# Weight tiles stored as they lie on chip, and a new order of the modulation tiles, in a two-block transformer kernel on one Trainium2 core

## What is computed

```python
# first block, per layer; sc = silu(c), c has 1024 entries
mod = sc @ w_mod[layer] + b_mod[layer]          # w_mod: 1024 x 6144 a layer
shift1, scale1, gate1, shift2, scale2, gate2 = split(mod, 6)
h = rmsnorm(x, g_attn) * (1 + scale1) + shift1
x = x + gate1 * mixer(h)      # h @ w_in, 16 heads of three kinds of attention, @ w_out
h = rmsnorm(x, g_mlp) * (1 + scale2) + shift2
u, g = split(h @ w_up, 2)     # 1024 x 5632
x = x + gate2 * ((silu(conv(g)) * u) @ w_down)  # 2816 x 1024
# second block, per layer
x = x + mixer2(rms_norm(x)) @ w_out_2           # w_in_2: 1024 x 2336, w_uq_2, w_ukv_2
x = x + expert_choice_moe(rms_norm(x))          # 16 experts, three 1024 x 1024 matrices each
```

## Time and profile before

| | us |
|---|---|
| median of 3 runs | 1885.98 |
| range of these | 1884.85 to 1887.53 |
| profiled execution: its own time | 1892.49 |
| profiled execution: span of the trace | 1890.6 |
| PE busy | 1609.9 (85%) |
| DVE busy | 762.4 (40%) |
| ACT busy | 312.3 (17%) |
| POOL busy | 190.2 (10%) |

### The profile page before, as it was taken

The page is one execution under the profiler, slowest core; times in us unless marked ns, Lnnn a source line. Parts: engine busy times, 40 slices in busy tenths (PEclk is TensorE's granted clock), DMA queues, the critical chain, the costliest instruction groups (busy, mean ns, idle before and its releaser), DMA issues.

```text
span 1890.6 us, 24872 instructions
## 1 busy us (share of the span) xinstructions
PE 1609.9 (85%) x10540; PEld 924.4 (49%) x10540; DVE 762.4 (40%) x1518; ACT 312.3 (17%) x820; POOL 190.2 (10%) x177
## 2 busy tenths in 40 slices
PE   8999999998999999999875856767999875866757
PEld 3456998443589964474332322322474432232322
DVE  5776687768637676666000100002576000000001
ACT  2161111021511201262000000002252000000000
POOL 0020052000214410320000000000220000000000
PEclk9999999999999999999987978979999996878979
DMA  9985996443566443747999999999946999999998
GB/s 369 371 320 178 326 345 226 134 162 149 190 218 195 179 154 118 228 179 315 424 433 428 429 431 422 434 429 403 296 179 272 425 432 428 429 430 424 432 430 342
DMA packets 152386, 600.52 MB, mean 318 GB/s; under 512 B 22368, under 2 KB 81248, under 8 KB 127712
## 3 DMA queue, kind: packets, MB, share of 16 engines
q1 hardware_dynamic: 152046, 598.58, 80.6%
q10 hardware_dynamic: 242, 0.53, 0.1%
HBM read 595.28 MB, written 3.82 MB: 317 GB/s over the span
## 4 chain that ended last, share of the span: by engine, by line
PE 60%; DMA 24%; another core or an unknown queue 7%; SPq 4%; DVE 2%; ACT 1%; issue 1%; POOL 0%; DVEq 0%; ACTq 0%
DMA far<-in_w_gate 13%; PE ps L1740 11%; PE ps L1377 10%; PE ps L1403 7%; DMA far<-in_w_down 6%; PE ps L1337 4%; PE ps L1446 4%; PE ps L1205 3%; PE ps L1287 3%; PE ps L1760 3%; PE ps L1618 3%; PE ps L1477 3%; DMA ring<-in_w_gate 2%; PE ps L1053 2%; DMA ring<-in_w_mod 2%
## 5 line engine op out<-in xcount | busy, mean ns | idle before, releaser
L1740 PE MATMUL ps<-ring,near 128*32 128x256 f32 x2560 | 192.2, 467 | 96.1 <-DMA ring<-in_w_up 48.2
L3458 DVE TENSOR_TENSOR near<-ps,near 128x512 f32<-128x512 f32 x16 | 10.7, 671 | 488.8 <-PE ps L1740 488.8
L1740 PEld LDWEIGHTS ps<-ring,near 128*32 128x32 f32 x2560 | 94.8, 133 | 187.1 <-DMA ring<-in_w_up 54.0
L2538 DVE CUSTOM_DVE_ANT_0 ring<-ring,far 128x1024 f32<-128x1024 f32 x96 | 120.2, 1301 | 42.5 <-DMA ring<-in_w_mod 42.4
L1760 PE MATMUL ps<-far,near 128*32 128x512 f32 x448 | 94.4, 673 | 49.1 <-DMA far<-in_w_down 49.1
L1740 PE MATMUL ps<-far,near 128*32 128x256 f32 x1024 | 82.3, 492 | 48.9 <-DMA far<-in_w_gate 25.3
L1377 PE MATMUL ps<-near,ring 128*128 128x128 f32 x960 | 115.5, 276 | 0.0
L1377 PEld LDWEIGHTS ps<-near,ring 128*128 128x128 f32 x960 | 111.9, 193 | 0.1
L1337 PE MATMUL ps<-near,ring 128*128 128x128 f32 (+1 forms) x704 | 99.3, 303 | 0.0
L1337 PEld LDWEIGHTS ps<-near,ring 128*128 128x128 f32 x704 | 94.0, 191 | 5.9 <-issue 1.0
L3474 DVE COPY near<-ps 128x512 f32<-128x512 f32 x8 | 5.5, 691 | 210.8 <-PE ps L1760 209.0
(11 more groups left out here) (369 smaller groups left out, 2451.1 us busy)
## 6 DMA issues: line engine op xcount, KB each, us to landing
ring<-in_w_gate SPq DMA_DIRECT2D x22, 4096.0 KB, 48.6
ring<-in_w_up SPq DMA_DIRECT2D x14, 4096.0 KB, 52.8
far<-in_w_down SPq DMA_DIRECT2D x14, 4096.0 KB, 52.9
ring<-in_w_up SPq DMA_DIRECT2D x44, 1024.0 KB, 11.9
ring<-in_w_mod SPq DMA_DIRECT2D x20, 2048.0 KB, 14.2
far<-in_w_gate SPq DMA_DIRECT2D x8, 4096.0 KB, 49.2
ring<-in_w_down SPq DMA_DIRECT2D x8, 4096.0 KB, 52.4
near<-in_w_down SPq DMA_DIRECT2D x8, 4096.0 KB, 52.4
```

Source lines behind the costliest of these rows:

```text
L1740: last = mm(ps[2 * part + e // 2][j * CAP:(j + 1) * CAP, e % 2 * 2 * P:(e % 2 + 1) * 2 * P], xsT[:, k, e * CAP:(e + 1) * CAP], expert_row( ...
L2538: nc.vector.tensor_tensor_reduce(v, v, csilb, 1.0, cc1(l, "b_mod", o, 1), ALU.mult, ALU.add, col)\
```

## The change

First, each weight outside the experts is stored on the host tile by tile, so that a partition's share of a tile is one run in DRAM: 16 KB for a whole tile, 8 KB or 4 KB for the pieces of the head. One DMA loads a tile where there were two (`up`, `head_mods`, pieces of `in` in the second block, `w_uq_2` with `w_ukv_2`). The forget gate's columns become 192 bytes a partition and the router's weights 1 KB. The same bytes are moved.

Second, the mod tiles take other places in the order of loads and of reads. In layer 0, one mod tile fewer is read ahead of the attention (five, tiles 4 to 8), tile 9 and `ab` come behind it, and the tiles behind that move by one; the two halves of tile 10 stand between the residuals. Loads of mod tiles behind the attention alternate with the up tiles. In layer 1, the reading of tile (1,4) moves behind `forget_log`.

```diff
-MOD_AT = {3: (4, 5), 4: (6, 7), 5: (8, 9)}
-MOD_READ = {2: (4,), 3: (5,), 4: (6, 7), 5: (8, 9)}
+MOD_AT = {3: (4,), 4: (5,), 5: (6, 7, 8, 9)}
+MOD_READ = {3: (4,), 4: (5, 6), 5: (7, 8)}
...
-MOD_AFTER = ({("in", LAST_IN): (10,), ("out", 1): (11,), ("up", 0): (12,), ("up", 1): (13,), ("up", 2): (14, 15), ("up", 3): (16,),
-              ("up", 4): (17, 18), ("up", 8): (19,)}, {("in", LAST_IN): (0, 1), ("out", 1): (2, 3)})
-MOD_WHOLE = {0: (15,), 1: (16,), 2: (17,), 3: (18,)}
-MOD_PARTS = {6: (19, range(0, 2)), 7: (19, range(2, 4))}
+MOD_AFTER = ({("in", LAST_IN): (10,), ("out", 1): (11,), ("up", 1): (12, 13), ("up", 2): (14,), ("up", 3): (15,),
+              ("up", 4): (16,), ("up", 5): (17,), ("up", 6): (18,), ("up", 7): (19,)}, {("in", LAST_IN): (0, 1), ("out", 1): (2, 3)})
+MOD_WHOLE = {0: (14,), 1: (15,), 2: (16,), 3: (17,)}
+MOD_PARTS = {5: (18, range(0, 2)), 6: (18, range(2, 4)), 7: (19, range(0, 2)), 8: (19, range(2, 4))}
...
             def mod_tile(t):
 
                 L, _, j = B1_TILES[t]
-                v = a["w_mod"][L, j * N:(j + 1) * N, :]
-                src = v.rearrange("(p n) k -> p n k", n=4) if j // 2 in (2, 5) else v.rearrange("(n p) k -> p n k", p=P)
-                sp.dma_start(slot_at(t).rearrange("p (n k) -> p n k", n=4), src).then_inc(arrived[b1_slot(t)], 16)
+                sp.dma_start(slot_at(t), a["w_mod"][L, j]).then_inc(arrived[b1_slot(t)], 16)
...
-                ks = slice(2 * h, 2 * h + 2)
-                src = a["w_in"][0, :, IN1_ORDER[i] * N:(IN1_ORDER[i] + 1) * N].rearrange("(k p) n -> p k n", p=P)
+                v = slice(2 * h * N, 2 * (h + 1) * N)
                 sem = arrived[b1_slot(t)] if h == KD // 2 - 1 else sems[HEAD_ROWS[HEAD_IN + h - 1 if h else i]]
-                sp.dma_start(slot_at(t).rearrange("p (k n) -> p k n", k=KD)[:, ks, :], src[:, ks, :]).then_inc(sem, 16)
+                sp.dma_start(slot_at(t)[:, v], a["w_in"][0, IN1_ORDER[i], :, v]).then_inc(sem, 16)
...
-                sp.dma_start(fgate[:, l * KD * CH:(l + 1) * KD * CH].rearrange("p (k n) -> p k n", k=KD),
-                             a["w_in"][l, :, IN1:IN1 + CH].rearrange("(k p) n -> p k n", p=P)).then_inc(sems["rows_loaded"], 16)
+                sp.dma_start(fgate[:, l * KD * CH:(l + 1) * KD * CH], a["w_forget"][l]).then_inc(sems["rows_loaded"], 16)
...
                 elif kind == "up":
-                    for half in range(2):
-                        o = half * DFF + j * 256
-                        src = a["w_up"][L, :, o:o + 256].rearrange("(k p) n -> p k n", p=P)
-                        sp.dma_start(d8[:, :, half * 256:half * 256 + 256], src).then_inc(sem, 16)
+                    sp.dma_start(dst, a["w_up"][L, j]).then_inc(sem, 16)
...
                     weights_sum("t4", 1)
-                    modulation(0, range(0, 1))
                     joined(3, 0)
-                    modulation(0, range(1, 3))
                     joined(4, 0)
                     rotate("A", 16, 16)
...
                     forget_log()
+                    modulation(0, range(0, 1))
                     joined(3, 1)
+                    modulation(0, range(1, 3))
                     joined(4, 1)
...
-                if L == 0:
-                    ab(0, 1, "g_mlp")
-
...
-                modulation(2 if L else 10)
+                modulation(2 if L else 9)
+                if L == 0:
+                    ab(0, 1, "g_mlp")
                 dve.wait_ge(sems["gate_loaded"], 32 * L + 16)
                 out_residual(0, 0)
-                if L:
-                    modulation(3, range(0, 2))
+                modulation(3 if L else 10, range(0, 2))
                 out_residual(0, 1)
                 norm_stream(which, 0)
-                modulation(3 if L else 11, range(2, 4) if L else range(0, 2))
+                modulation(3 if L else 10, range(2, 4))
                 out_residual(1, 0)
...
+    arrays["w_up"] = layers(lambda l: _np.stack([rows_first(_np.concatenate([i["w_up"][l][:, o:o + 256] for o in (256 * j, DFF + 256 * j)], axis=1))
+                                                 for j in range(UPT)]))
```

More of the change, by code:

```diff
@@ L443, in two_blocks @@
         for t, tile in enumerate(B1_TILES):
-            seen[b1_slot(t)] += 32 if tile[1] == "up" or 2 <= t < FAST else 16
+            seen[b1_slot(t)] += 16
             B1_ARR.append(seen[b1_slot(t)])
@@ L447, in two_blocks @@
             for t, (kind, j) in enumerate(B2_TILES):
-                seen[b2_slot(t)] += 48 if kind == "small" else 16 * len(IN2_TILES[j][1]) if kind == "in" else 16
+                seen[b2_slot(t)] += 32 if kind == "small" else 16
                 B2_ARR.append(seen[b2_slot(t)])
@@ L813, in _ @@
                                  rpad[0:84, :].unsqueeze(1).to_broadcast([84, GRID, P])).then_inc(sems["rpb_copied"], 16)
[L814 to L815 removed]
+                    sp.dma_start(router[:, 0:DEPTH * KD * EXP], a["w_router_2"]).then_inc(sems["router_loaded"], 16)
                 slot_free(t)
@@ L820, in _ @@
                     load_gate(0, 0)
-                if (L, kind, j) == (1, "mod", 3):
+                if (L, kind, j) == (0, "up", 3):
                     store_gate(0, 1, first_block[0].at("b1_mod_read", 8))
-                if (L, kind, j) == (1, "mod", 6):
+                if (L, kind, j) == (0, "up", 4):
                     load_gate(0, 1)
@@ L2892, in _ @@
                 if L == 0:
-                    modulation(11, range(2, 4))
+                    modulation(11, range(0, 2))
                 out_residual(1, 1)
@@ L2896, in _ @@
                 if L == 0:
-                    modulation(12, range(0, 2))
+                    modulation(11, range(2, 4))
                 evac_stream(which, 1, 24)
                 if L == 0:
-                    modulation(12, range(2, 4))
+                    modulation(12)
                     modulation(13)
-                    modulation(14)
                 def conv(j):
@@ L3573, with rows_first @@
         "g_final": i["g_final"].reshape(1, D), "c": i["c"].reshape(1, D),
-        "w_mod": _np.ascontiguousarray(i["w_mod"].transpose(0, 2, 1)),
     }
-    for n in ("w_in", "w_out", "w_up", "w_down", "w_in_2", "w_out_2", "w_uq_2", "w_ukv_2",
-              "w_router_2", "conv_w_2"):
-        arrays[n] = i[n]
-    arrays["w_out_2"] = _np.ascontiguousarray(i["w_out_2"].reshape(DEPTH, KD, P, D)[:, OUT2_ROWS]).reshape(DEPTH, D, D)
+    def rows_first(v):
+        return v.reshape(v.shape[0] // P, P, v.shape[1]).transpose(1, 0, 2).reshape(P, -1)
@@ new lines, in outputs_first, with head_first, layers @@
+    def outputs_first(v, q):
+        if q // 2 in (2, 5):
+            return v.T[q * N:(q + 1) * N].reshape(P, 4 * D)
+        return v.T[q * N:(q + 1) * N].reshape(4, P, D).transpose(1, 0, 2).reshape(P, 4 * D)
+    def head_first(v, q):
+        return v.T[0:2 * D].reshape(2, KD, P, D).transpose(2, 1, 0, 3)[:, 2 * q:2 * q + 2].reshape(P, 4 * D)
+    def layers(f):
+        return _np.ascontiguousarray(_np.stack([f(l) for l in range(DEPTH)]))
+    arrays["w_mod"] = layers(lambda l: _np.stack([head_first(i["w_mod"][l], q) if l == 0 and q < FAST else outputs_first(i["w_mod"][l], q)
+                                                  for q in range(12)]))
@@ new lines @@
+    arrays["w_in"] = layers(lambda l: _np.stack([rows_first(i["w_in"][l][:, j * N:(j + 1) * N]) for j in range(IN1 // N)]))
+    arrays["w_forget"] = layers(lambda l: rows_first(i["w_in"][l][:, IN1:IN1 + CH]))
+    arrays["w_out"] = layers(lambda l: _np.stack([rows_first(i["w_out"][l][:, j * N:(j + 1) * N]) for j in range(2)]))
+    arrays["w_up"] = layers(lambda l: _np.stack([rows_first(_np.concatenate([i["w_up"][l][:, o:o + 256] for o in (256 * j, DFF + 256 * j)], axis=1))
+                                                 for j in range(UPT)]))
@@ new lines @@
+    arrays["w_down"] = layers(lambda l: rows_first(i["w_down"][l]))
+    arrays["w_in_2"] = layers(lambda l: _np.concatenate(
+        [rows_first(_np.concatenate([i["w_in_2"][l][:, o:o + w] for o, w in pieces], axis=1)) for _, pieces in IN2_TILES], axis=1))
+    out2 = i["w_out_2"].reshape(DEPTH, KD, P, D)[:, OUT2_ROWS].reshape(DEPTH, D, D)
+    arrays["w_out_2"] = layers(lambda l: _np.stack([rows_first(out2[l][:, j * N:(j + 1) * N]) for j in range(2)]))
+    arrays["w_small_2"] = layers(lambda l: _np.concatenate([rows_first(i["w_uq_2"][l]), i["w_ukv_2"][l]], axis=1))
@@ L3580 @@
+    arrays["w_router_2"] = _np.ascontiguousarray(_np.concatenate([rows_first(v) for v in i["w_router_2"]], axis=1))
+    arrays["conv_w_2"] = i["conv_w_2"]
     for n in ("w_gate_2", "w_up_2", "w_down_2"):
```

42 lines of the change are left out of this document (12 added, 30 removed).

## The result

The changed kernel takes 1876.5 us (median of 7 runs, 1875.19 to 1881.22) where the kernel before, measured beside it, takes 1887.53 (7 runs). The ratio is 0.9941, interval 0.9927 to 0.9956: 11.1 us less, 8.3 to 13.8. That lies in the range 1861 to 1877, but only 0.5 us inside its upper end, and outside the 1865.5 to 1872.5 that the forecast itself had; it is 8.1 us above its 1868.4, of which 1.5 us is the base (1885.98 then, 1887.53 beside this run). The profiled execution took 1876.95 us, its span is 1874.9.

A forecast was written before the change was run, and what follows sets the result against it. Expert weights' DMA bounds 889 to 1310, untouched; before it, PE's stalls are the gain. 1.5 + 3.5 + 4.1 + 8.5 = 17.6 us off the median 1885.98 gives 1868.4 us, range 1861 to 1877 (the forecast's own 1865.5 to 1872.5).

The forecast's parts named there:

- the second rival: A new DVE wait in up tiles or fifth `in` step takes half back; 1874 to 1878 us, chance 0.16.
- the four places: PE's stalls ahead of 889: the head, then at 70, 245 and 430 us; 17.6 us to gain in all.
- Stall 4: At 430, layer 1: DVE waits for mod tile (1,4); moving `modulation(0)` behind `forget_log` gains 8.5 us, bounds 6.8 and 8.5.
- Stall 2: At 70, `in` loop: DVE copies the third result late behind `modulation(4)`; the new order gains 3.5 us.
- Stall 3: At 245, first up tile by seven products lands late; packing and earlier issue gain 4.1 us, bounds 2.3 and 4.1.
- The head: Before 28.91, PE waits 1.17 and 0.71 us for `w_in`; faster transfers gain 1.5 us, bounds 0 and 2.9.
- What is added: Mod reads moved between residuals, behind attention, into up tiles 5 to 8: hidden; four half tiles cost 0, bound 4 us.
- The clock: Lower PE clock behind stalls 2, 3 and 4, taken as their price: 1.45, 1.74 and 1.63 us.
- The first rival: Order alone works, runs of 512 B suffice, the head gives 0: 16.1 us gained, 1869.9 us, chance 0.12.

The follow-up runs named there:

- e1_unchanged: The kernel before, run and traced a second time with nothing changed: 1886.56 us, ratio 1.000.
- e7_mod0_only: The kernel before with one edit, the reading of mod tile (1,4) moved behind the forget gate's logarithm: 1878.54 us.
- e3_layout_only: The kernel before with only the packed tiles and their loads, order of mod tiles as before: 1879.46 us.
- the spread one: The changed kernel with mod tile 18's first half ahead of the rows' sums, its second in up tile 6, tile 19 in up tiles 8 and 9: 1873.5 us.
- e5_pool_small: The changed kernel with POOL's sums of layer 0's up tiles 6 to 10 cut to 1 of 128 columns: stage "seven" 75.04 us instead of 78.50.
- e8_fill: The kernel before with unread 128x512 products filling PE's waits at stalls 2, 3 and 4: 1886.40 us against 1887.07 beside it.

## Why the prediction was right or wrong

**Where the time went.** Right: the gain was to be had only where PE stands still ahead of 889, and the experts' rate stayed. The start of the experts moved by 16.3 us between the two first traces (889.60 to 873.31), the span by 15.7. Against e1_unchanged it moved by 8.0. The medians, 11.1, lie between.

That the time lies in the range is in part luck. It fell into the second rival's band (1874 to 1878, chance 0.16), and its mechanism was at work; the outer range held it by 0.5 us in one measurement and by 0.1 in the other (1876.90). The direction and three of the four places were right by their causes.

**Stall 4**, 8.5 us: right; 8.5 by e7_mod0_only in the median, where the interval of 5.5 to 11.5 makes the exact hit luck, and 7.3 to 9.0 by the traces.

**Stall 2**, 3.5 us: gone, and its size is 2.7 against e1_unchanged and 4.0 against the first trace. I gave it to the order; e3_layout_only shows that the layout removes it as well. The margins in the later steps of the `in` loop held: PE has no wait on DVE there. (The 13.8 us for an `in` tile were added up wrongly: 2 × 7.13 − 0.2 is 14.1, and the rival has 13.7. Nothing hangs on it.)

**Stall 3**, 4.1 us: gone, as said by both parts, and either alone is enough. Up tile 5 has landed when POOL's sums begin at 220.38, before 230 as forecast. It is worth 2.5 us in a stage without a dip (77.48 to 75.03) and 4.2 with one (79.24).

**The head**, 1.5 us: nothing came. The rate rose as said (350 to 387) and the hole closed, but the two waits stayed at 1.3 and 0.6, which is the lower bound (0) that I had written down. The `w_in` waits of the head are 0.9 to 1.9 us in traces with the old layout and 0.4 to 2.1 with the new one, so no part of the 1.5 can be seen. The forget gate's loads were to be issued in under 1 us; packed they take 6.94:

```profile
27.16 6.94 SPq L798 DMA_DIRECT2D far<-in_w_forget  x2
```

The earlier trace rows had 6.41. The number of rows does not set that time. `in` tile 3 was issued earlier all the same, at 37.11 instead of 49.47, because SP got through its other issues sooner.

**What is added**, counted as 0: the step that failed, in its last part, the four half tiles. (The additions behind the attention were free as said: from the first product of `out` to the first of `up` it is 33.16 us before and 33.17 after, and from layer 1's first down product to the first expert product 211.18 in both.) "Such a tile lasts 12.50 us on PE and DVE is busy for 10.21 with a half tile in it, so 2.3 us are left." There was no such margin in the trace of before. What counts is not DVE's busy time in a window but its round: DVE works through an up tile in a fixed order, in which it also stands still (1.22 us in each round for ACT). A round is read from one instruction to the same one of the next tile. In the kernel before, with the mod reads between:

```profile
259.42 1.79 DVE L2915 SCALAR_TENSOR_TENSOR near<-far,near 128x255 f32<-128x255 f32 x4 [1.22 <-ACT near L2036]
...
263.36 1.28 DVE L2538 CUSTOM_DVE_ANT_0 ring<-ring,far 128x1024 f32<-128x1024 f32 x1
...
272.79 1.79 DVE L2915 SCALAR_TENSOR_TENSOR near<-far,near 128x255 f32<-128x255 f32 x4 [1.22 <-ACT near L2036]
...
276.70 1.27 DVE L2538 CUSTOM_DVE_ANT_0 ring<-ring,far 128x1024 f32<-128x1024 f32 x1
...
277.90 2.28 DVE L2538 CUSTOM_DVE_ANT_0 ring<-ring,far 128x1024 f32<-128x1024 f32 x1
...
285.91 1.79 DVE L2915 SCALAR_TENSOR_TENSOR near<-far,near 128x255 f32<-128x255 f32 x4 [1.22 <-ACT near L2036]
...
296.94 1.79 DVE L2915 SCALAR_TENSOR_TENSOR near<-far,near 128x255 f32<-128x255 f32 x4 [1.22 <-ACT near L2036]
```

The two rounds with a half tile take 13.37 and 13.12 us, both over PE's 12.50; the next, without one, takes 11.03 and pays the debt back. My window 265.8 to 278.3 hid this: it starts behind the reads at 263 and takes in 1.67 us of those at 276. In the changed kernel four rounds in a row have a half; the last three of them:

```profile
252.72 1.79 DVE L2888 SCALAR_TENSOR_TENSOR near<-far,near 128x255 f32<-128x255 f32 x4 [1.22 <-ACT near L2012]
...
265.84 1.79 DVE L2888 SCALAR_TENSOR_TENSOR near<-far,near 128x255 f32<-128x255 f32 x4 [1.22 <-ACT near L2012]
...
279.96 1.79 DVE L2888 SCALAR_TENSOR_TENSOR near<-far,near 128x255 f32<-128x255 f32 x4 [1.22 <-ACT near L2012]
...
295.57 1.79 DVE L2888 SCALAR_TENSOR_TENSOR near<-far,near 128x255 f32<-128x255 f32 x4 [1.22 <-ACT near L2012]
```

These rounds take 13.12, 14.12 and 15.61 us: one read beside POOL's sums, then two, then two and DVE's own sums as well (2.02 and 1.75 instead of 1.23 and 0.68). The more DVE falls behind, the more of its work lies beside POOL's sums. Against 3 × 12.50 it is 5.35 us behind; banks ahead cover a part, and the stage grows by 3.47 (78.50 − 75.03), near my bound of 4. With small POOL sums the same rounds take 12.29, 12.51 and 12.51, PE's own pace (from 249.89, 262.18, 274.69 and 287.20). The mechanism is that of the second rival, in one place of its two and without its loss in clock: the clock reads 1.00 from 252 to 300.

**Behind it** the stage "down" is 0.35 us longer in the order-only and the changed kernel (67.33 after 66.97) and in the spread one (67.24). It is 66.97 in e5_pool_small, which has the same order and differs only in POOL's sums, so these have a part in it; in the changed kernel it lies in one group of 12 products, 5.67 us from 320.41 where the kernel before has 5.31, and no wait is recorded for it.

**The clock.** I added 1.45 + 1.74 + 1.63 = 4.8 us, as though every execution paid it. The rows behind e1_unchanged show that it is paid in some, and I took 17.6, a sum from an execution with all dips, off a median. With the head, the overrun and "down" put right the sum is 17.6 − 1.5 − 3.5 − 0.35 = 12.2 with all dips, and 7.4 with none; the 11.1 measured lies between. But e8_fill, which had none in its trace, has nearly the median of the kernel before, so the median may pay little for dips, and then some 3 us of the 11.1 (by its interval at least 0.9) have no term; their source is open. For the spread version, without the 3.5, it is 15.7 and 10.9, and it has 13.6 (1873.5 against 1887.1). The lower bounds of my terms did leave the clock out ("no clock back" for stall 4), but the value taken never did.

**The first rival**, that packing gives nothing, is refuted as a whole: the layout alone gives 7.4 us. Which part of the layout gives it (the length of the runs, the forget gate's loads, one DMA a tile in place of two) no run tells apart. With the order in place it adds little, 1878.04 to 1876.5, which the intervals don't separate.

## What to carry to other kernels

Before work is added to an engine in a loop, measure its round, from an instruction to the same one of the next pass, and hold it against the round of the engine that it serves; busy time in a window leaves out the waits that belong to the round, and its borders can cut off the very instructions that it is read for. Price a moved instruction from a row beside the same neighbours as it will have: here the same read had 1.28 us alone and 2.28 when it began behind one of POOL's sums, both in one trace. And a sum taken from one execution holds that execution's luck with the clock: keep the clock's price as a range between none and all of it.

## What the runs showed of the hardware

- A DVE read of two 128x1024 operands takes 1.28 us, and 2.28 when it begins behind one of POOL's two-operand sums; DVE's two sums for the products go from 0.69 to 1.75 and from 1.23 to 2.02. POOL's sums, two in 2.49 us while DVE stands still (from 220.38), take 3.48 to 4.52 in the up tiles from 256 on.
- Such instructions of DVE and POOL take turns, and one that finds the other engine idle takes its usual time: a DVE sum of 2.29 us took 7.72 when a POOL sum of 5.62 had begun 0.04 us ahead of it, and POOL's took 7.35 when DVE had begun 0.42 us ahead.
- The same kernel with nearly the same idle times on PE (2.0 and 2.3, 2.0 and 2.2 us) shows clock 0.89 and 0.91 behind them in one execution and 1.00 in another. A dip that lay ahead of a wait for DVE cost nothing: 1.70 us more on PE, 1.70 us less wait.
- Contiguous tiles of 16 KB a partition pass at 424 to 436 GB/s where 1 KB rows passed at 355.
- SP's issue of two forget gate loads takes 6.4 us with 1024 rows of 24 bytes each and 6.9 us with 128 rows of 192 bytes.
